# Seven seams of a float32 transformer block: TensorE's, ScalarE's, VectorE's and SyncE's order around them

## The reference

```python
x = layer_norm(ALPHA * x + 0.5 * swiglu(x, ffn1_w1, ffn1_w3, ffn1_w2), ln1_g, ln1_b)
q_lat, kv_lat, k_rope, u, g_a, g_b = split(x @ w_in)
c_q, c_kv = rms_norm(q_lat, q_norm_g), rms_norm(kv_lat, kv_norm_g)
y_a = attention(c_q, c_kv, k_rope) @ w_o_attn
y_b = s5_branch(u, ...) @ w_o_ssm           # a state space model in both directions, then a GLU
x = layer_norm(ALPHA * x + (sigmoid(g_a) * y_a + sigmoid(g_b) * y_b) @ w_out, ln2_g, ln2_b)
x = layer_norm(ALPHA * x + 0.5 * swiglu(x, ffn2_w1, ffn2_w3, ffn2_w2), ln3_g, ln3_b)
x = layer_norm(ALPHA * x + sigmoid(x @ ple_w_gate) * (p @ ple_w_proj), ln4_g, ln4_b)
# second block: x is normed and modulated to h, and mix(h) is added
va, za, bb, bc, bv, zb, ca, cg, zc, dv, zd = split(h @ w_in)
ya = rglru(va)                               # 4-tap convolution both ways, gates, a scan
yb = bb * depthwise_conv(bc * bv)
u = depthwise_conv(ca * sigmoid(cg), 31 taps)
yc = silu(layer_norm(u)) @ c_pw
yd = pool(dv) ...
out = concat(ya * silu(za), yb * silu(zb), yc * silu(zc), yd * silu(zd)) @ w_out
return rms_norm_2(x + gate * out, final_g)
```

## Time and profile before

| what | value |
|---|---|
| three executions | 3119.57, 3123.17, 3123.41 us; median 3123.17 us |
| the profiled execution | 3120.53 us, of which the span of instructions is 3118.7 us |
| mean granted clock of TensorE | 0.997 of full speed |
| PE busy | 3075.9 us (99%), 15342 matmuls |
| DVE busy | 2316.6 us (74%) |
| ACT busy | 1225.1 us (39%) |
| POOL busy | 56.2 us (2%) |
| DMA | 250.21 MB, mean 80 GB/s |

### The profile page before, as it was taken

The page is one execution under the profiler, slowest core; times in us unless marked ns, Lnnn a source line. Parts: engine busy times, 40 slices in busy tenths (PEclk is TensorE's granted clock), DMA queues, the critical chain, the costliest instruction groups (busy, mean ns, idle before and its releaser), DMA issues.

```text
span 3118.7 us, 38749 instructions
## 1 busy us (share of the span) xinstructions
PE 3075.9 (99%) x15342; PEld 2501.0 (80%) x15342; DVE 2316.6 (74%) x3975; ACT 1225.1 (39%) x1894; POOL 56.2 (2%) x49
## 2 busy tenths in 40 slices
PE   8999999999999999999999999999999999999998
PEld 6887888887988887777888888888877788788887
DVE  6777767777859678888578766766776789789636
ACT  4233323335242455554243232222365634534414
POOL 0000000000000001130000000000000000000000
PEclk9999999999999999999999999999999999999999
DMA  3222221223333351012212111111211321122242
GB/s 132 75 70 79 77 66 62 73 69 128 106 96 136 125 198 47 8 55 108 108 42 68 41 54 61 48 54 48 68 62 46 115 77 64 48 70 102 81 169 75
DMA packets 89252, 250.21 MB, mean 80 GB/s; under 512 B 8560, under 2 KB 24816, under 8 KB 87536
## 3 DMA queue, kind: packets, MB, share of 16 engines
q1 hardware_dynamic: 89072, 247.73, 23.5%
HBM read 203.65 MB, written 44.04 MB: 79 GB/s over the span
## 4 chain that ended last, share of the span: by engine, by line
PE 92%; DVE 5%; ACT 2%; DMA 1%; issue 0%; SPq 0%; DVEq 0%; ACTq 0%
PE PS L580 90%; PE PS L585 2%; DVE WS L2306 1%; DVE COLB L3113 0%; DMA RAW<-in_W 0%; DVE TMP L2306 0%; DVE X L2314 0%; ACT WS L1405 0%; ACT X L1405 0%; DVE TMP L2310 0%; DVE PT L3131 0%; DVE XC L2314 0%; ACT XS L1405 0%; DVE XS L2314 0%; ACT TMP L1405 0%
## 5 line engine op out<-in xcount | busy, mean ns | idle before, releaser
L580 PE MATMUL PS<-XS,WS 128*128 128x512 f32 (+1 forms) x6480 | 1511.1, 390 | 14.6 <-DVE XS L2306 9.2
L580 PEld LDWEIGHTS PS<-XS,WS 128*128 128x128 f32 x6480 | 1209.0, 188 | 285.4 <-issue 23.4
L580 PE MATMUL PS<-HS,WS 128*128 128x512 f32 x2208 | 510.4, 390 | 3.1 <-DVE TMP L2306 2.7
L580 PEld LDWEIGHTS PS<-HS,WS 128*128 128x128 f32 x2208 | 413.6, 188 | 92.0 <-DVE TMP L2306 3.5
L2306 DVE TENSOR_TENSOR WS<-RAW,WS 128x512 fp32r<-128x512 f32 (+1 forms) x398 | 347.4, 881 | 176.7 <-ACT WS L1405 176.1
L1405 ACT ACTIVATE WS<-RAW 128x512 fp32r<-128x512 f32 (+1 forms) x398 | 307.7, 779 | 401.9 <-PE PS L580 351.4
L2306 DVE TENSOR_TENSOR X<-PS,X 128x512 f32<-128x512 f32 x272 | 184.3, 689 | 102.3 <-PE PS L580 102.2
L2306 DVE TENSOR_TENSOR TMP<-TMP,PS 128x512 f32<-128x512 f32 x304 | 203.8, 683 | 69.5 <-PE PS L580 65.6
L580 PE MATMUL PS<-T,WS 128*128 128x512 f32 x960 | 230.6, 389 | 0.0
L580 PEld LDWEIGHTS PS<-T,WS 128*128 128x128 f32 x960 | 180.2, 188 | 37.4
L1405 ACT ACTIVATE TMP<-PS 128x512 f32<-128x512 f32 x144 | 85.2, 596 | 292.8 <-PE PS L580 276.3
(11 more groups left out here) (343 smaller groups left out, 3536.4 us busy)
## 6 DMA issues: line engine op xcount, KB each, us to landing
RAW<-in_W SPq DMA_DIRECT2D x263, 512.0 KB, 3.5
RAWX<-in_W SPq DMA_DIRECT2D x30, 512.0 KB, 3.5
DC<-TMP SPq DMA_DIRECT2D x32, 256.0 KB, 2.1
X<-in_xT SPq DMA_DIRECT2D x8, 512.0 KB, 8.9
DX<-X SPq DMA_DIRECT2D x2, 2048.0 KB, 8.4
DCZ<-CA SPq DMA_DIRECT2D x8, 512.0 KB, 4.3
DGA<-TMP SPq DMA_DIRECT2D x16, 256.0 KB, 2.2
DGB<-TMP SPq DMA_DIRECT2D x16, 256.0 KB, 2.9
```

The costliest lines, as they stand in the source:

```text
L580: done = d.matmul(out, l, r, start=first, stop=last)
```

## The change

The arithmetic stays the same but for the last norm. In `latents` the products (1,0) and (2,0) go in a pair, tile by tile, with the norm's mean ahead of tile 7 of the pair (before: at tile 6 of the second), and the sums of squares of kv come one product later. In `embed` the gate products of m = 0 and 1 go in a pair with the mean at tile 6, and the two embedding products behind them. On ACT `factor_slot` stands ahead of `biased` in both halves of the last norm of the first block, and PE's spread of half 1 comes at tile 2 of a plane instead of tile 4. On SP `loads(129)`, which is eight loads, stands ahead of two `load_gate` and two `load_latent`. On DVE the two multiplies UU of the first channel tile stand ahead of the taps of XC1. In the last norm the parts 1 and 2 are summed by quarters of 64 tokens on 32 partitions each, the reciprocal is taken of 128x64 elements, and PE spreads it back to PSUM, from where `scale_out` reads it.

```diff
@@ -785,32 +785,35 @@
             us = {i: w.take() for i in (1, 2, 0, 3, 4, 5)}
             for n, (i, h) in enumerate(LATENTS):
                 use = ("lat", i, h)
-                if n != 6:
+                if n not in (1, 6):
                     banks.take(use, (ac, *use))
                 if n == 5:
                     flush()
-                    i2, use2 = LATENTS[6][0], ("lat", *LATENTS[6])
+                if n in (0, 5):
+                    i2, use2 = LATENTS[n + 1][0], ("lat", *LATENTS[n + 1])
                     banks.take(use2, (ac, *use2))
                     e.wait_ge(w_hi(us[i]), w_lo(us[i]), w_hi(us[i2]), w_lo(us[i2]), *banks.free(use), *banks.free(use2))
                     for k in range(8):
+                        if (n, k) == (0, 7):
+                            hook()
                         e.wait_ge(ac("xs", "ln1", k, h), ve("xs", "ln1", k, h))
                         done = mms(group3(bank(*use), [(blk(us[i], 128 * k), xs_pair(k, h))], first=k == 0, last=k == 7))
                         if k == 7:
                             done.then_inc(*mm.inc(*use))
                         done = mms(group3(bank(*use2), [(blk(us[i2], 128 * k), xs_pair(k, h))], first=k == 0, last=k == 7))
                     done.then_inc(*mm.inc(*use2))
...
-                elif n != 6:
+                elif n not in (1, 6):
                     e.wait_ge(w_hi(us[i]), w_lo(us[i]), *banks.free(use))
                     for k in range(8):
-                        if (n, k) in ((1, 6), (2, 4), (3, 4), (4, 0)):
+                        if (n, k) in ((2, 4), (3, 4), (4, 0)):
                             hook()
                         e.wait_ge(ac("xs", "ln1", k, h), ve("xs", "ln1", k, h))
                         done = mms(group3(bank(*use), [(blk(us[i], 128 * k), xs_pair(k, h))], first=k == 0, last=k == 7))
                     done.then_inc(*mm.inc(*use))
                 if h:
                     release(us[i])
-                if n in (6, 7):
-                    square_sum("kv", n - 6, 2, lambda k: tmp("sq", "kv", n - 6, k))
+                if n in (7, 8):
+                    square_sum("kv", n - 7, 2, lambda k: tmp("sq", "kv", n - 7, k))
...
-                banks.take(use, (ac, *use))
-                product8(us[m], h, use, "ln3", beside=True,
-                         within={1: (4,), 2: (4,), 3: (4,), 4: (0,), 8: (4,), 9: (4,), 10: (4,), 11: (4,), 12: (4,), 13: (0,)}.get(n))
+                if n == 0:
+                    pair = [("pg", *EMBED[j]) for j in range(2)]
+                    for j, other in enumerate(pair):
+                        banks.take(other, (ac, *other))
+                        e.wait_ge(w_hi(first[j]), w_lo(first[j]), *banks.free(other))
+                    for k in range(8):
+                        if k == 6:
+                            hook()
+                        e.wait_ge(ac("xs", "ln3", k, 0), ve("xs", "ln3", k, 0))
+                        for j, other in enumerate(pair):
+                            done = mms(group3(bank(*other), [(blk(first[j], 128 * k), xs_pair(k, 0))], first=k == 0, last=k == 7))
+                            if k == 7:
+                                done.then_inc(*mm.inc(*other))
+                elif n > 1:
+                    banks.take(use, (ac, *use))
+                    product8(us[m], h, use, "ln3", beside=True,
+                         within={2: (4,), 3: (4,), 4: (0,), 8: (4,), 9: (4,), 10: (4,), 11: (4,), 12: (4,), 13: (0,)}.get(n))
...
-                        if h == 0 and (i, k) in ((0, 6), (1, 4), (2, 4), (4, 4)):
+                        if h == 0 and (i, k) in ((0, 6), (1, 4), (2, 4), (4, 2)):
...
+            spread_out(1)
             row_squares(2)
+            spread_out(2)
 
         def row_squares(p):
 
             use = ("sq", "out", p)
-            banks.take(use, (ac, "rs", "out", p))
-            out = bank(*use)[:, 0:512 if p == 0 else 256]
-            e.wait_ge(ve("sqs", 6 if p else 7, p), *banks.free(use))
-            done = mms([(out, ones[:], held_part(p), True, p == 0)])
-            if p:
-                e.wait_ge(ac("sq", "out", p, 3))
-                done = mms([(out, ones[:], tmp("sq", "out", p, 3)[:, 0:256], False, True)])
+            e.wait_ge(ve("sqs", 6 if p else 7, p))
+            if p == 0:
+                banks.take(use, (ac, "rs", "out", p))
+                e.wait_ge(*banks.free(use))
+                done = mms([(bank(*use), ones[:], held_part(p), True, True)])
+            else:
+                banks.take(use, (ve, "fin", p, 3))
+                e.wait_ge(*banks.free(use))
+                for i, src in enumerate((held_part(p), tmp("sq", "out", p, 3))):
+                    if i:
+                        e.wait_ge(ac("sq", "out", p, 3))
+                    done = mms([(bank(*use)[32 * g:32 * g + 32, 0:64], ones[:, 0:32], src[:, 64 * g:64 * g + 64], i == 0, i == 1)
+                                for g in range(4)])
             done.then_inc(*mm.inc("sq", "out", p, 7))
+
+        def spread_out(p):
+
+            e.wait_ge(ve("rs", "out", p), dma("const")("cols"))
+            mms([(bank("sq", "out", p)[:, 64 * g:64 * g + 64], ident[:, 32 * g:32 * g + 1].to_broadcast([128, 128]),
+                  tmp("rs", "out", p)[:, 0:64], True, True) for g in range(4)]).then_inc(*mm.inc("rb", "out", p))
 
...
-            tmps.take(use, (ve, *(end or use)))
+            tmps.take(use, (mm, "rb", name, h) if width == 64 else (ve, *(end or use)))
...
             gate(11)
+            factor_slot("h", 0)
             biased(0)
-            factor_slot("h", 0)
...
                     h_squares(1)
+                    factor_slot("h", 1)
                     biased(1)
-                    factor_slot("h", 1)
...
-                release(*us[:3 if ct else 2])
-                for h in range(2):
-                    e.wait_ge(ac("cg", ct, h), mm("ca", ct, h), ve("cv", ct - 1) if ct else ve("pad", "uu"))
-                    tt(UU[:, 15 + 512 * h:527 + 512 * h], tmp("cg", ct, h), bank("ca", ct, h), ALU.mult).then_inc(
-                        *ve.inc("uu", ct, h))
+                    if n == (1 if ct else 0):
+                        if ct:
+                            release(*us[:3])
+                        for h in range(2):
+                            e.wait_ge(ac("cg", ct, h), mm("ca", ct, h), ve("cv", ct - 1) if ct else ve("pad", "uu"))
+                            tt(UU[:, 15 + 512 * h:527 + 512 * h], tmp("cg", ct, h), bank("ca", ct, h), ALU.mult).then_inc(
+                                *ve.inc("uu", ct, h))
+                if ct == 0:
+                    release(*us[:2])
                 release(*us[:3])
...
+            def rstd_quarters(p):
+
+                r = tmp("rs", "out", p)[:, 0:64]
+                e.wait_ge(ac("rs", "out", p))
+                d.reciprocal(r, r).then_inc(*ve.inc("rs", "out", p))
+
             def scale_out(p, g):
 
                 a, b = FINISH[p][g]
-                x, r = X[:, a:b, out_part(p)], held_part(p)
-                e.wait_ge(ve("rs", "out", p), ac("fg", b - 1, 1 if a > 3 and p else p))
+                x, r = X[:, a:b, out_part(p)], bank("sq", "out", p)[:, 0:256] if p else held_part(p)
+                e.wait_ge(mm("rb", "out", p) if p else ve("rs", "out", p), ac("fg", b - 1, 1 if a > 3 and p else p))
                 tt(x, x, r.unsqueeze(1).to_broadcast([128, b - a, r.shape[-1]]), ALU.mult).then_inc(*ve.inc("fin", p, g))
 
...
+        loads(129)
         e.wait_ge(mm("glu", 3, 1))
         load_gate(0)
         load_gate(1)
         e.wait_ge(ve("glm", 3, 1))
         for i in (4, 5):
             load_latent(i)
-        loads(129)
```

More of the change, by code:

```diff
@@ L2252, in square @@
                 if p == 2 and m == 1:
-                    root("out", 1, 1024, RMS_EPS, mm("sq", "out", 1, 7), width=256)
+                    root("out", 1, 1024, RMS_EPS, mm("sq", "out", 1, 7), width=64)
                 e.wait_ge(ac(*use))
@@ L2271, in outputs @@
                     square(m, p, *((ve, "sqs", 4 + m, p) if m < 3 else (mm, "sq", "out", p, 7)))
-            root("out", 2, 1024, RMS_EPS, mm("sq", "out", 2, 7), width=256)
+            root("out", 2, 1024, RMS_EPS, mm("sq", "out", 2, 7), width=64)
         for h in range(2):
@@ L3627, in outputs @@
                     if p == 2 and m == 1:
-                        rstd("out", 1, held_part(1), width=256)
+                        rstd_quarters(1)
             for p in (1, 2):
                 if p == 2:
-                    rstd("out", 2, held_part(2), width=256)
+                    rstd_quarters(2)
                 for g in range(4):
```

## The result

The changed kernel takes 3132.91 us (median of six executions, 3130.25 to 3138.48) against 3123.12 us before (3119.57 to 3123.56): ratio 1.0037, 95% interval 1.0026 to 1.0048. The medians lie 9.8 us apart, so it is slower, by little. Its profiled execution has a span of 3131.0 us, 12.3 us more than before. The forecast was 3135, slower.

What follows compares the result with a forecast made beforehand. PE was taken as the bound, busy 3075.9 of 3118.7 us. Seam terms 0.8 + 3.9 - 4.95 + 1.2 + 6.0 + 6.6 - 0.2 summed to +13.4, giving 3135 us; 8-in-10 range 3123 to 3141.

Steps and rivals of the forecast that it cites:

- Latents and embedding: the mean is set by DVE: Latents +0.8 us, embedding +3.9: PE waits in one piece for DVE's addition into HELD, 2.6 and 4.0 us.
- The clock behind the new waits: Lower PE clock behind long waits costs 1.7 us (latents), 2.5 (embedding), 1.6 (SP's queue), 2.9 (wait for PB).
- SP's order: SP's queue: GBR issued after the eight loads, so PE waits for DVE's multiplications with GBR: +6.0 us (3.0 to 8.5).
- The root of half 0: Root ahead of ACT's biases: spread 3.2 us earlier, lower clock gone, until DVE sets the mean: -4.95 us.
- Half 1: Root ahead of the biases must wait for PE's sums, ACT idles, HX and XS come later: +1.2 us.
- UU: Second UU waits for PE's matmuls, delaying casts and loads; PE waits 5.8 us for PB: +6.6 us.
- The last norm: Reciprocal falls from 1.75 to about 0.5 us, a spread with 0.8 us hand-over is added: -0.2 us.
- nothing takes the place of the waits: Rival, all seams: each wait goes because DVE, ACT and SP have room, 14 us gained, 3109 us; chance 10%.
- the mixer or SP have room: Two rivals: SP's reordering is free, about 3129 us, 14%; UU's delay is made good before PB, about 3127.5, 12%.
- the clock stays up: Rival: no lower PE clock behind the new waits, +4.7 us in sum, about 3126.5 us; chance 12%.
- both rooms at once: Rival: SP's reordering free and the mixer's delay made good together, -0.5 us, 3121 to 3124 us; chance 6%.
- the cases within 6 us: Outcomes of 3117 to 3129.4 us, not told from no change; the forecast gave them 27% together.

Runs made afterwards that it cites:

- sp_back: The changed kernel with SP's eight loads put back behind the two GBR and two LR loads: 3124.96 us, ratio 1.0013 to the kernel before.
- uu_only: The kernel before with both UU of the first channel tile ahead of the taps of XC1, nothing else: 3127.79 us, ratio 1.0021.
- latents_late: The kernel before with the latents' pair, its mean at 54 matmuls, and kv's sums of squares one product later: 3118.80 us, ratio 0.9990.
- embed_only: The kernel before with the pair of gate products in the embedding as in the change, nothing else: 3125.65 us, ratio 1.0012.
- embed_late: The kernel before with the embedding's pair, its mean at 54 matmuls, sums and spread later too: 3120.78 us, ratio 0.9997.
- last_mid2: The kernel before with the last norm by quarters, its last reciprocal between the multiplications of the part before: 3120.06 us, ratio 0.9998.
- half1_only2: The kernel before with half 1's root ahead of the biases and the spread two tiles earlier, nothing else: 3123.59 us, ratio 1.0006.
- root_only: The kernel before with the root of half 0 ahead of the biases on ACT, nothing else: 3116.15 us, ratio 0.9985.
- uu0_only: The kernel before with only the first of the two UU ahead of the taps of XC1: 3120.29 us, ratio 0.9998.
- the fitted version: The kernel before with root_only, uu0_only, latents_late, last_mid2 and embed_late (spread two tiles earlier) together: 3107.74 us, ratio 0.9960.

## Why the prediction was right

**The direction and the size** were right: of seven seams only the root of half 0 gains anything to speak of. The forecast sum was +13.4, the traces have +11.6 in the seams. That it came so close is in part luck: the clock's terms were 0.9 and 1.4 too high, SP's 1.2 too low, and the clock's terms differ between executions of the same code.

**Latents and embedding: the mean is set by DVE.** Right. The forecast said waits of 2.6 and 4.0 us for HELD, the trace has 2.45 and 3.81, and the mean of the embedding is exactly as late as the mark ahead of it (2281.56 - 2273.24 = 8.32). The two fitted pairs show it from the other side: with 54 matmuls ahead of the mean the same pairs gain.

**The clock behind the new waits** was mis-sized. I had read the cost as growing with the wait: 1.7 behind 2.36 us, 2.9 behind 4.71, so 2.5 behind 4.0 and 2.9 behind 5.8. In the changed kernel it is 3.0 - 1.4 = 1.6 behind 3.81 and 4.9 - 3.4 = 1.5 behind 5.82. The windows show how. The first two rows are the last 3.4 us of the wait of 5.82 and the 3.4 us behind it; the next two the last 1.1 us of the 4.71 before and the 5.8 us behind it; the last two the same at the 3.81 of sp_back:

```profile
2490.50:2493.90 3.40, 0.00 (x0) 0.00 (x1) 3.33 (x5) 3.27 (x6) 0.47 (x1) 0.52 0.21 87
2493.90:2497.30 3.40, 3.37 (x8) 2.72 (x9) 3.36 (x5) 0.84 (x2) 0.00 (x0) 0.50 0.22 29
...
2366.70:2367.80 1.10, 0.00 (x0) 0.00 (x0) 0.95 (x1) 0.09 (x1) 0.00 (x0) 0.54 0.80 324
2367.80:2373.60 5.80, 5.77 (x18) 4.90 (x19) 1.42 (x2) 3.63 (x5) 0.00 (x0) 0.50 0.04 17
...
2270.20:2271.70 1.50, 0.00 (x0) 0.00 (x0) 1.47 (x4) 1.50 (x4) 0.00 (x0) 0.53 0.86 295
2271.70:2277.00 5.30, 5.30 (x11) 3.49 (x12) 4.27 (x7) 4.33 (x9) 0.00 (x0) 0.50 0.36 111
```

In all three the clock is at its lower level for some 6.8 us. Only what lies behind the wait costs time, about half of its length: of the 6.8 us half fell into the wait of 5.82, but only 1.1 into the 4.71 and 1.5 into the 3.81 of sp_back. Behind the 3.81 of the changed kernel the lower level lasted 3.4 us, and behind the 2.44 of sp_back it did not come at all. So the same seam costs 1.6 or 2.5 of clock in the embedding and 1.6 or nothing in the latents, and the length of the wait doesn't order these. This is the step of the forecast that failed: by it the term of the embedding was 0.9 too high and that of UU 1.4, and where a term agreed (1.7 in the latents, +3.9 for the embedding of sp_back) that was chance. What decides when the clock falls stays open. The rule of the Trainium skill (TensorE: Matmul & The Clock Gate, HAM oscillation), that an engine which has idled runs its next matmuls cold, holds in the changed kernel, where each of the five new waits above 2 us ahead of the last norm has a stretch below full clock at its end or just behind it, but not in sp_back, where 2.44 and 2.46 us have none; how much a wait takes had to be measured.

**SP's order.** Right in each step: the issue of GBR behind the last load (forecast 1136.6 for the second, measured about 1137.7, of which 1.12 are the lateness ahead), DVE idle until it lands, PE waiting for DVE. It was 1.2 too low: the first GBR took 6.1 us to land and so came when I had the second one land, and all four multiplications stood behind it where I had counted two; they end at 1143.51 + 2.57 = 1146.1, 5.7 later than before beyond the 1.12 ahead (forecast 4.4). The half clock ahead of it (ZG's 48 matmuls took 13.91 us instead of 11.26) cost nothing, since PE arrived before the data anyway; it only made PE's wait 2.47 us where I had said about 4. The clock behind that wait cost 7.2 - 5.7 = 1.5 (forecast 1.6). sp_back takes the whole away.

**The root of half 0.** Right in both parts: -3.28 at the spread, and the rest from the half clock that went, until DVE sets the mean (forecast 4.95, 5.2 measured, 5.0 alone).

**Half 1.** Right: ACT idles 3.33 us ahead of the root in both traces, +1.2 forecast, +1.2 and 1.1 measured.

**UU.** Right in each step but the clock: stall 5.29 (forecast 5.2), the high casts' end 3.4 late (3.7), the wait for PB 5.82 (5.8).

**The last norm.** +0.1 instead of -0.2: the reciprocal fell to 0.55 us as forecast, but DVE stood idle for 1.20 us behind it, for the way over PE, instead of 0.8.

**The rivals.** That nothing takes the place of the waits is refuted at each seam. That the mixer or SP have room is refuted by uu_only and sp_back. That the clock stays up is refuted in the changed kernel at each of those five waits, but sp_back has it at two places. Two of my sums were off without weight for the result: both rooms at once give 13.4 - 6.0 - 6.6 - 1 = -0.2, not -0.5, and the chances of the cases within 6 us (6, 12 and half of 26) add up to 31%, not 27%.

## What to carry to other kernels

Before a wait is taken away, ask what the waiting engine needs next and when that is ready: at most of these seams it was an engine that worked without a gap, and PE only waited elsewhere, in one piece and mostly with a lower clock behind it. Count the matmuls up to the moment at which the other engine is done and put the dependent instruction there: the same two pairs that cost 3.5 us (2.8 in sp_back) gained 5.8 when the mean stood 12 to 18 matmuls later. An instruction moved ahead in a queue has to be looked at for what it waits for itself: the first UU was ready and gained 1.1 us, the second was not and cost 4.9; one root was ready, the other not; and eight loads that each wait held up four transfers that were ready.

## What I had not expected

One stretch that no edit touches takes three different times. ZG's 48 matmuls begin 18.0 us behind the first row of CX, after a wait for a load and one for a low cast. In sp_back, uu_only and latents_late they take 11.1 to 11.2 us, in embed_only, embed_late, last_mid2 and half1_only2 12.7 to 12.8 and in root_only 13.9, with waits that differ by a few tenths at most. In sp_back, shown above, they take 11.16 behind a wait of 2.46; here half1_only2 and root_only:

```profile
1125.98 12.74 PE L580 MATMUL PS<-ZG,WS 128*128 128x512 f32 x48 [2.47 <-issue]
1126.00:1129.40 3.40, 3.40 (x8) 2.72 (x9) 3.19 (x8) 1.06 (x1) 0.00 (x0) 0.50 0.53 188
...
1125.04 13.93 PE L580 MATMUL PS<-ZG,WS 128*128 128x512 f32 x48 [3.01 <-issue]
```

It is the granted clock: 1.00 over the whole stretch in sp_back, 0.50 for the first 3.4 us in half1_only2 and for 6.8 us in root_only, the first 0.9 of them still in the wait. In sp_back and half1_only2 the waits ahead are the same within 0.03 us. In the kernel before, uu0_only and the fitted version the lower clock comes earlier, behind a wait of 1.90 to 2.36 us for the load, and ZG runs at full clock. At the mark behind the gates this makes up to 2.5 us that come and go with nothing changed, which is as large as most effects of this study; only the marks within one trace could tell the seams apart, and where a seam's cost holds a term of the clock, even they give it for one execution only.
